# A two-layer decoder trunk: attention units that hold half the blocks of both heads, early scores, and W_o in two passes

## The reference, cut to what matters

```
q = rms_norm(h @ w_q, per head of 64) ; three groups g: (window, dilation) = (128,1), (512,4), (2048,16); 16 heads
for each group: s = q k^T under a causal band on blocks ; m = max s ; p = exp(s - m) ; l = sum p ; o_g = (p/l) v ; lse_g = m + log l
o = sum_g softmax_g(lse_g) * o_g ; y = o @ w_o ; x = x + y, then the last FFN
```

## Time and profile before

| what | us |
|---|---|
| median of 3 runs (2720.28 to 2726.48) | 2724.66 |
| the profiled execution, its own time | 2723.88 |
| its span, first to last instruction | 2722.2 |
| TensorE busy with matmuls | 2606.3 (96%) |
| VectorE, ScalarE, POOL busy | 815.6, 965.2, 983.4 |
| granted TensorE clock, mean over the span | 0.969 |

### The profile page before, as it was taken

One profiled execution on the slowest core, in us unless ns is written; L12 is line 12 of the kernel. 1 busy time (PEld: TensorE's weight loads), 2 busy tenths in 40 slices (PEclk: granted clock), 3 DMA queues, 4 the chain that ended last, 5 costly groups with the idle time before them and its releaser, 6 DMA issues.

```text
span 2722.2 us, 47151 instructions
## 1 busy us (share of the span) xinstructions
PE 2606.3 (96%) x18986; PEld 2209.2 (81%) x18986; DVE 815.6 (30%) x1329; ACT 965.2 (35%) x1598; POOL 983.4 (36%) x473
## 2 busy tenths in 40 slices
PE   6999999988898999999999999999997997999999
PEld 5888886767776888888898988888897886888887
DVE  3222014454553222201331022220324555322201
ACT  3232223533443333322443233331343652333321
POOL 3444442322222344444334444444342000444442
PEclk8999999988988999999999999999998998999999
DMA  3333331200001233232334333232222230233221
GB/s 125 94 99 94 99 100 61 83 29 4 4 4 34 75 103 100 93 100 93 109 117 161 132 116 100 93 100 93 85 93 78 71 94 8 85 101 97 95 98 64
DMA packets 180815, 230.39 MB, mean 85 GB/s; under 512 B 16472, under 2 KB 119032, under 8 KB 180664
## 3 DMA queue, kind: packets, MB, share of 16 engines
q1 hardware_dynamic: 180664, 228.20, 26.0%
HBM read 213.47 MB, written 14.68 MB: 84 GB/s over the span
## 4 chain that ended last, share of the span: by engine, by line
PE 93%; DVE 2%; ACT 2%; issue 1%; POOL 0%; SPq 0%; DMA 0%; DVEq 0%; ACTq 0%; POOLq 0%
PE bank L332 20%; PE bank L333 20%; PE bank L334 20%; PE bank L339 6%; PE bank L340 5%; PE bank L341 5%; PE bank L1977 2%; PE bank L1955 1%; PE bank L1148 1%; PE bank L1261 1%; PE bank L1231 1%; PE bank L1279 1%; PE bank L1702 1%; PE bank L1940 1%; PE bank L1463 1%
## 5 line engine op out<-in xcount | busy, mean ns | idle before, releaser
L307 POOL TENSOR_TENSOR w_lo<-w_raw,w_hi 128x1024 fp32r<-128x1024 f32 x376 | 904.8, 2411 | 1470.3 <-ACT w_hi L302 1469.7
L302 ACT ACTIVATE w_hi<-w_raw 128x1024 fp32r<-128x1024 f32 x376 | 395.6, 1058 | 1078.0 <-PE bank L334 904.3
L332 PE MATMUL bank<-xg_hi,w_hi 128*128 128x512 f32 x1408 | 551.0, 391 | 9.7 <-POOL w_lo L307 6.8
L334 PE MATMUL bank<-xg_hi,w_lo 128*128 128x512 f32 x1408 | 550.0, 391 | 0.0
L333 PE MATMUL bank<-xg_lo,w_hi 128*128 128x512 f32 x1408 | 550.0, 391 | 0.0
L332 PEld LDWEIGHTS bank<-xg_hi,w_hi 128*128 128x128 f32 x1408 | 265.8, 189 | 65.6 <-POOL w_lo L307 6.8
L334 PEld LDWEIGHTS bank<-xg_hi,w_lo 128*128 128x128 f32 x1408 | 265.6, 189 | 55.4
L333 PEld LDWEIGHTS bank<-xg_lo,w_hi 128*128 128x128 f32 x1408 | 265.7, 189 | 55.2
L332 PE MATMUL bank<-hid_hi,w_hi 128*128 (+1 forms) x704 | 274.3, 390 | 0.0
L333 PE MATMUL bank<-hid_lo,w_hi 128*128 (+1 forms) x704 | 273.9, 389 | 0.0
L334 PE MATMUL bank<-hid_hi,w_lo 128*128 (+1 forms) x704 | 273.9, 389 | 0.0
(11 more groups left out here) (292 smaller groups left out, 3312.5 us busy)
## 6 DMA issues: line engine op xcount, KB each, us to landing
w_raw<-in_ffn_w_in SPq DMA_DIRECT2D x352, 256.0 KB, 2.9
w_raw<-in_ffn_w_out SPq DMA_DIRECT2D x176, 256.0 KB, 2.7
w_raw<-in_w_kv SPq DMA_DIRECT2D x96, 256.0 KB, 3.1
w_raw<-in_rwkv_w_rkv SPq DMA_DIRECT2D x48, 256.0 KB, 2.9
w_raw<-in_attn_w_q SPq DMA_DIRECT2D x48, 256.0 KB, 3.0
k_dram<-stage SPq DMA_DIRECT2D x6, 1024.0 KB, 4.8
v_dram<-stage SPq DMA_DIRECT2D x6, 1024.0 KB, 5.6
keys<-k_dram SPq DMA_DIRECT2D x24, 256.0 KB, 4.2
```

The source lines that it names most:

```text
L302: act.activation(w_hi[:, s, :], w_raw[:, s, :], ACT.Copy).then_inc(w_hi_ready, 1)
L307: pool.tensor_tensor(w_lo[:, s, :], w_raw[:, s, :], w_hi[:, s, :].bitcast(F32), ALU.subtract).then_inc(w_lo_ready, 1)
L332: pe.matmul(o, hi, x_hi, start=start, stop=False)
L334: return pe.matmul(o, lo, x_hi, start=False, stop=stop)
```

## The change

1. **Units.** A unit is now (pair, f, half): both heads of a pair with two of the four blocks. The heads' scores are separate matmuls that contract over partitions 0 to 63 and 64 to 127 and write different banks; the padded queries, `head_half` and their tensors go. Value products alternate between the heads, which write the two halves of the partitions. VectorE, not ScalarE, copies the finished output bank.
2. **Keys and constants early.** `keys` lies where it doesn't overlap the projection's operands; SP loads keys of pairs 0 and 1 after the query projection's third group, VectorE builds the masks there. TensorE scores units 0 and 1 after the last projection chunk, before it transposes the last group; their maxima and unit 0's exponentials stand ahead of the last copies to `q_all`.
3. **W_o in two passes.** A chunk is two rows k by 512 columns. The first pass goes to banks 4 to 7 (m = 4 to 7), row k as soon as pair k is weighted, between the spreading of the pairs, which uses banks 0 to 3; spreading is a transpose of TensorE and ScalarE makes its source. The second pass goes to banks 0 to 3.
4. **Update order.** The last FFN's update goes through m = 4, 5, 6, 7, 0, 1, 2, 3: the first four may be updated after the first pass. VectorE runs two `new_x` ahead of the rest instead of four.

The core of the diff:

```diff
+                if ph["groups"] is Q_GROUPS and gi == 2:
+                    for i in range(2):
+                        sp.wait_ge(stored[i], 16 * (len(KV_GROUPS) // 2))
+                    for q in range(2):
+                        load_keys(sp, q)
...
+            if ph["groups"] is Q_GROUPS:
+                pe.wait_ge(attn_const, ATTN_CONSTS)
+                pe.wait_ge(staged_odd, 2 * (2 * KEYS_GROUPS - 1))
+                pe.wait_ge(staged_even, 2 * (2 * KEYS_GROUPS - 1))
+                for i in range(2):
+                    scores_pe(pe, i)
...
+                if kind == "q" and last_group:
+                    exps_act(act, 0)
...
+                if kind == "q" and gi == 2:
+                    attn_consts_dve(dve)
+                if kind == "q" and gi == len(ph["groups"]) - 1:
+                    for i in range(2):
+                        negmax_dve(dve, i)
...
+        UNITS_A = [(q, f, half) for q in range(PAIRS_H) for f in range(2) for half in range(2)]
         NU = len(UNITS_A)
+        WO_ORDER = (4, 5, 6, 7, 0, 1, 2, 3)
...
+            for hh in range(2):
                 if i >= 2:
+                    pe.wait_ge(p_ready, 4 * (i - 2) + 2 * hh + 2)
+                pe.matmul(score_bank(i, hh)[:, :], ident_bf[:, :], masks_bf[:, 2 * f + half], start=True, stop=False)
+            for b in (2 * half, 2 * half + 1):
+                blk = slice(b * P, (b + 1) * P)
+                if f == 0:
+                    parts = [(0, (max(b - 1, 0), b + 1))]
+                else:
+                    parts = [(1, (b, b + 1)), (2, (b, b + 1))]
+                for g, (k0, k1) in parts:
+                    at = (b % 2) * 256 + (P if g == 2 or f == 0 and b == 0 else 0)
+                    for hh in range(2):
+                        rows = slice(hh * HD, (hh + 1) * HD)
+                        last = pe.matmul(score_bank(i, hh)[:, at:at + (k1 - k0) * P], q_all[rows, q, g, blk],
+                                         keys[rows, q % 2, g, k0 * P:k1 * P], start=False,
+                                         stop=b % 2 == 1 and g != 1)
+                        if b % 2 == 1 and g != 1:
+                            last.then_inc(scores_done, 1)
...
+            for e in range(2):
+                b = 2 * half + e
                 for kb in range(2):
+                    if f == 0 and b == 0 and kb == 0:
+                        continue
+                    for hh in range(2):
+                        cols = slice(hh * HD, (hh + 1) * HD)
+                        v = values[:, q % 2, 0, b - 1 + kb, cols] if f == 0 else values[:, q % 2, 1 + kb, b, cols]
+                        last = pe.matmul(bank[6 + f][cols, b * P:(b + 1) * P], v, probs_t[:, i % 2, hh, 2 * e + kb],
+                                         start=kb == 0 or (f == 0 and b == 0), stop=kb == 1)
             last.then_inc(pv_done, 1)
...
+            for i in range(2, NU + 2):
+                if i == 2:
+                    turn_pe(pe, 0)
                 if i < NU:
                     scores_pe(pe, i)
+                pv_pe(pe, i - 2)
+                if i <= NU:
+                    turn_pe(pe, i - 1)
+                if i == NU:
+                    pe.wait_ge(p_ready, 4 * NU)
+                    for b in range(TB):
+                        last = pe.matmul(bank[0][:, b * P:(b + 1) * P], select[:, b],
+                                         sums[:, 1].rearrange("p b s h -> p (b s h)"), start=True, stop=True)
+                    last.then_inc(converted, 1)
+
+            c0 = ph["c0"] + len(Q_GROUPS) * QKV_CHUNKS
+
+            def wo_row(j, kk, k, m0):
+                pe.wait_ge(w_lo_ready, c0 + j + 1)
+                for m in range(m0, m0 + 4):
+                    last = products(pe, bank[m][:, :], (c0 + j) % SLOTS, kk * COLS + m % 4 * P,
+                                    o_hl[:, k, 0], o_hl[:, k, 1], k == 0, k == KT - 1)
+                    if k == KT - 1 and m % 4 != 3:
+                        last.then_inc(out_done, 1)
+                if kk == 1:
+                    last.then_inc(w_used, 1)
+
+            for q in range(2):
+                spread_weights_pe(pe, q)
+            for q in range(PAIRS_H):
+                if q + 2 < PAIRS_H:
+                    spread_weights_pe(pe, q + 2)
+                if q == 0:
+                    for i in range(2):
+                        pe.wait_ge(turn_read[i], NU)
+                        pe.wait_ge(u_copied[i], PAIRS_H)
+                pe.wait_ge(o_lo_ready, q + 1)
+                wo_row(q // 2, q % 2, q, 4)
+            pe.wait_ge(weighted, 3 * PAIRS_H)
+            for k in range(KT):
+                wo_row(SLOTS + k // 2, k % 2, k, 0)
...
+            split_hi(act, c)
+
+            def spread(q):
+                if q >= 2:
+                    act.wait_ge(w_spread, q - 1)
+                for f in range(2):
+                    act.activation(spread_w[:, q % 2, f], joint[:, 1 + f, :, 2 * q:2 * q + 2].unsqueeze(3).to_broadcast(
+                        [P, TB, 2, HD]), ACT.Copy).then_inc(spread_source, 1)
+
+            act.wait_ge(merged, 10)
+            act.wait_ge(pv_done, NU)
+            for q in range(2):
+                spread(q)
+            for q in range(PAIRS_H):
+                if q + 2 < PAIRS_H:
+                    spread(q + 2)
+                act.wait_ge(weighted, 3 * (q + 1))
+                act.activation(o_hl[:, q, 0], q_all[:, q, 0], ACT.Copy).then_inc(o_hi_ready, 1)
+                if q in (5, 7) and c + q // 2 - 1 < CHUNKS:
+                    split_hi(act, c + q // 2 - 1)
+            split_hi_run(act, c + 3, min(KT - 3, CHUNKS - c - 3))
...
+            def low(q):
+                dve.wait_ge(o_hi_ready, q + 1)
+                dve.tensor_tensor(o_hl[:, q, 1], q_all[:, q, 0], o_hl[:, q, 0].bitcast(F32),
+                                  ALU.subtract).then_inc(o_lo_ready, 1)
+
             for q in range(PAIRS_H):
                 dve.wait_ge(w_spread, q + 1)
                 for f in range(2):
                     dve.tensor_tensor(q_all[:, q, f], q_all[:, q, f], bank[2 * (q % 2) + f][:, :],
                                       ALU.mult).then_inc(weighted, 1)
+                if q > 0:
+                    low(q - 1)
                 dve.wait_ge(weighted, 3 * q + 2)
                 dve.tensor_tensor(q_all[:, q, 0], q_all[:, q, 0], q_all[:, q, 1], ALU.add).then_inc(weighted, 1)
+            low(PAIRS_H - 1)
...
+                if i == KT - 1:
+                    dve.wait_ge(w_used, ph["c0"])
+                elif ph["order"] == IN_ORDER:
+                    dve.wait_ge(out_done, ph["outs"] + i + 1)
+                elif i == 3:
+                    dve.wait_ge(w_used, ph["c0"] - G_CHUNKS)
                 else:
+                    dve.wait_ge(out_done, ph["outs"] + i + 1 - i // 4)
...
+            first, ahead = (0, 4) if ph["order"] == IN_ORDER else (4, 2)
             if u is not None:
+                for i in range(first):
+                    new_x(i)
+                    if i > 0:
+                        low(i - 1)
+                        add_squares(i - 1)
+                if first:
+                    low(first - 1)
+                    add_squares(first - 1)
+                for i in range(first, first + ahead):
+                    new_x(i)
                 if u == 0:
                     dve.wait_ge(par_ready, 2)
+            for i in range(first, KT):
                 if p is not None:
+                    low(i)
+                if u is not None and i + ahead < KT:
+                    new_x(i + ahead)
                 if ph["ssq"] is not None:
+                    add_squares(i)
```

More of the change, by code:

```diff
@@ L379, in update_dve @@
                 if p is not None:
-                    low(m)
-                if u is not None and m + 4 < KT:
-                    new_x(m + 4)
+                    low(i)
+                if u is not None and i + ahead < KT:
+                    new_x(i + ahead)
                 if ph["ssq"] is not None:
-                    add_squares(m)
+                    add_squares(i)
         def update_act(act, ph):
             u, p, st = ph["x"], ph["prep"], ph["stat"]
-            for m in range(KT):
-                act.wait_ge(x_new, KT * u + m + 1)
+            for i, m in enumerate(ph["order"]):
+                act.wait_ge(x_new, KT * u + i + 1)
@@ L1919, in load_wo @@
-        def load_wo(sp, ph, k):
-            load_chunk(sp, ph["c0"] + len(Q_GROUPS) * QKV_CHUNKS + k, row_halves(a["attn_w_o"][0, k * P:(k + 1) * P, :]))
+            for j in range(SLOTS, KT):
+                load_wo(sp, ph, j)
+        def load_wo(sp, ph, j):
+            k, first = j % SLOTS * 2, 0 if j >= SLOTS else COLS
+            load_chunk(sp, ph["c0"] + len(Q_GROUPS) * QKV_CHUNKS + j, [
+                (a["attn_w_o"][0, (k + kk) * P:(k + kk + 1) * P, first:first + COLS],
+                 lambda slot, kk=kk: slot[:, kk * COLS:(kk + 1) * COLS]) for kk in range(2)])
@@ L1922, in scores_pe, with score_bank @@
```

(58 more changed lines are left out.)

240 lines of the change are left out of this document (85 added, 155 removed).

## The result

The changed kernel took 2657.3 us (median of 4 runs, 2649.14 to 2661.86) beside 2725.57 for the kernel before (4 runs, 2720.28 to 2729.8): ratio 0.9747, 95% interval 0.9714 to 0.9781. In a second comparison it took 2661.80 (5 runs) beside 2728.83 (9 runs): 0.9747, 0.9723 to 0.9771. It is 2.5% faster; both medians lie in the predicted range, 7 and 12 us above the predicted 2650.

What follows compares the result with a forecast made beforehand. TensorE, busy almost throughout, was taken as the bound. Units -46.8, entry -10.0, output projection -24.1 and FFN head +6.5 sum to -74.4 us from 2723.88, giving 2649.5, stated as 2650, own range 2636 to 2664 (0.67).

Steps and rivals of the forecast that it cites:

- Units, -46.8: Attention units, first transpose of probabilities to last value product: 106.4 us instead of 153.2, with 29 units at 3.40.
- rival 1: Value products: column halves do not overlap, 1.64 us a unit stays; +22 us, 2672; chance 0.13.
- rival 3: Units: nothing overlaps, units at 4.98 us, only entry and tail gain; 2695; chance 0.04.
- Three switches: Each unit: three changes between whole-array and half-array work, taken at 0.37 us in all.
- rival 2: Units: full drain at every switch, 0.78 us a unit instead of 0.37; +12 us, 2662; chance 0.12.
- The tail after the last scores: End of the units: reductions, exponentials, transpose, copy and value products after the last scores, 5.4 us.
- The rule against the change: Units: the Trainium skill's rule that changing tiling mode drains TensorE; by it the sum would be 12 us higher.
- Entry, -10.0: Last query projection product to first transpose of probabilities: gain 12.3 us, less 2.3 for work at the lower clock.
- Output projection, -24.1: Last value product to the end of the output projection: 63.4 us against 87.5, as 5.4+7.2+49.6+1.2.
- the 7.2 behind it: Output projection: spreading, transposes, products and splitting after the joint softmax until pair 0 can be projected, 7.2 us.
- Head of the FFN, +6.5: Last FFN's start: first product waits about 5.3 us for its low part, plus half a chance of lower clock (2.4).
- Rival 4: Units: the lower clock holds through them, kernel slower; +96 us, 2746; chance 0.04.

Runs made afterwards that it cites:

- run 1: Changed kernel with each unit's value products issued head by head instead of alternating: units 124.96 us, rhythm 3.88 for 3.49.
- run 2: Changed kernel with all score matmuls of head 0 ahead of those of head 1 instead of side by side: units 121.61 us.
- run 3: Changed kernel with value products and transposes cut in alternating halves, two more tiling switches a unit: units 121.18 us, rhythm 3.75 for 3.49.
- Run 4: Changed kernel with units 0 and 1 scored only after the query projection's transposes and last copies: entry 16.90 us instead of 12.93, units 112.08.
- run 8: Changed kernel with ScalarE's split of W_o chunk 3 moved behind pair 3: 2655.53 us, ratio 0.9730 to the kernel before.
- Run 5: Changed kernel with W_o in one pass of eight banks after all pairs are spread, new spreading kept: 2662.17 us, ratio 0.9755 to the kernel before.
- run 7: Changed kernel with ScalarE's splits of the last FFN's chunks 0 to 2 moved inside the update: 2652.72 us, ratio 0.9714 to the kernel before.

## Why the prediction was right, and where its sizes were off

The mechanisms named were those that the traces show, and the total fell inside the range. By its own steps, against the first execution (the sum was -74.4, the spans differ by 62.1):

- **Units, -46.8.** Without the slow start, whose cost the prediction had put under the entry, they took some 111.4 instead of 106.4. Overlap of row and column halves is full when heads alternate (1.02 for 1.89; runs 1 and 2), so rival 1 and rival 3 fall. For column halves this was a choice more than a reading: the 64 x 64 tiles of the earlier trace rows (L1148) lie in different row halves as well, so their halved time could come from the rows alone, and their 0.017 is above, not below, the 0.014 beside which it was put. Two terms were too small. Three switches were priced at 0.37. The chain shows 0.21 + 0.14 + 0.14 = 0.49, and run 3 gives 0.13 to 0.16 for each: above the 0.37, below the 0.78 of rival 2. With the waits of one unit in four the rhythm is 3.49, not 3.40: 29 x 0.09 = 2.6. The tail after the last scores took 7.5 (2205.74 to 2213.22), not 5.4: 2.1. It is 3.4 until ScalarE's copy is there, and then 4.1 of TensorE's own work, since value products, transposes and the sums' matmuls still stand ahead of the last value products.
- **The rule against the change.** A switch costs some 0.15 here (run 3). The Trainium skill, TensorEngine Tiling (Array Packing), Key Properties, says that a change of tiling mode drains TensorE; the trace agrees that there is a price, and shows it as a sixth of the work between two switches, not enough to turn the change.
- **Entry, -10.0.** -12.7 to the first transpose (predicted -12.3), and the lower clock after it cost 1.9 in one execution and nothing in the other (predicted 2.3). Run 4 shows the parts.
- **Output projection, -24.1.** -24.8. Two errors nearly cancel in it, which is luck. The first product of `W_o` came 14.2 after the last value product instead of 12.6, since the joint step took 2.30 instead of 0.36 (run 8; the 7.2 behind it were 7.4). From there the rest took 48.4 instead of 50.8 (49.6 and 1.2 for the clock): only five spreadings lie behind the first product, not six, with periods of 3.60 to 3.86, and the clock was 0.90 from 2226 to 2231. Run 5 adds what the prediction didn't ask: of these, 11.4 are the spreading's.
- **Head of the FFN, +6.5.** The wait was 6.33, predicted 5.3, for the reason given: ScalarE's splits ahead of the update (run 7). What the estimate left out is the first low part, which took 2.38 beside POOL's step instead of 0.74. The lower clock was put in at half a chance and 1.2; it came in both executions, after 6.3 us in which TensorE did nothing, and the FFN's first half took 4.2 to 4.6 longer: 0.50 from 2282 to 2288, and 0.76 again from 2306 to 2312, though TensorE had been busy throughout since 2288; why it fell a second time stays open. In proportion this is the largest error (11.1 for 6.5). Run 7, which removes the wait, gives 3.7 of it back.
- **Rival 4** (the lower clock through the units) did not come: 2.7 us of waits in 101, half of them in the tail, left the clock at 1.00.
- The part before the change ended 4.5 us later. The sum has no term for it; 4.4 of it were there at 927 us, in code that the change leaves alone.

Units 4.1 (with the entry), the FFN 4.6, the part before 4.5, less 0.7 for the output projection: these are the 12.4 or so between -74.4 and -62.1.

## What to carry to other kernels

Two matmuls that each use half of the array run at the price of one when they alternate in the queue; put a whole head's worth in a row and half of the gain or more is lost (1.51 and 1.64 here). A stage that ends earlier is worth only what the next one can take: before splitting a projection into passes, look at what stands in the queues ahead of its consumer, here three weight splits on ScalarE that held back 9.7 us until they were moved. And an instruction that looks like a delay on the critical engine may be filling a wait that another engine sets; the trace tells by what that engine would wait for next.

## What the runs showed of the hardware

- **How far halves overlap.** With eight records of one half ahead of it, the first record of the other half started beside the fifth (0.49 us after the first for column halves, 0.55 for row halves); with four ahead it started at once (0.013).
- **A switch between tilings** cost 0.13 to 0.16 us (run 3). Column halves with all 128 rows overlapped as fully as row halves (sixteen records in 1.02 and 1.09).
- **POOL stops VectorE.** VectorE operations with two operands in SBUF that began beside POOL's low-part step (2.34 to 2.41) took far longer: the two of the joint weights 2.30 instead of 0.36 together, the low part 2.38 instead of 0.74. They ended 0.2 and 0.6 us after POOL's step did. An operation with one operand in SBUF and one in a bank (L2191), begun at 2226.39 in run 8 beside a step of POOL that ran from 2226.35 to 2228.76, took its usual 0.68. The Trainium skill, SBUF — State Buffer, Who interferes with whom, says that the port pair which the two engines share is an exclusive lock, and that a VectorE instruction with two SBUF inputs contends with a GpSimd instruction that reads SBUF; the trace agrees.
- **The same kernel, two clocks.** After the wait at the entry the granted clock was 0.74 in one execution and 1.00 in the next. Effects of 2 us at such a place can't be read from one profile.
